# Attention work of two rounds in one group between runs of uncut projection tiles

## The chip, the cores and the metric

The kernel runs on one core of one Trainium2 chip. The metric is the device time of one execution in microseconds; less is better. Engines are named as in the profile: PE is TensorE's matmul side, DVE is VectorE, ACT is ScalarE, POOL is GpSimd, and SP is the queue that issues most transfers.

## The reference, cut to what matters

One decoder layer over 2048 tokens of width 1024, in float32. The changed part is the first sublayer:

```python
z = rms_norm(x, norm_g) @ w_in            # qa, ka, va, qr, kr, vr, gr, up
scores = einsum(qb, kk) * HEAD_DIM ** -0.5 + bias      # 128-token blocks: own and previous block
scores = where(valid, scores, NEG_INF)
m = maximum(scores.max(-1), sink)
p = exp(scores - m[..., None])
o = einsum(p, vv) / (p.sum(-1) + exp(sink - m))        # 6 query heads, 2 key/value heads
...
x = x + concat(o, retention(qr, kr, vr, gr), pool_mixer(up)) @ w_out
x = x + square(relu(rms_norm(x) @ w_up)) @ w_down
```

The retention part rotates `qr` and `kr` (rotary), and works on the same 128-token chunks.

## The kernel before

The mixer runs four passes (`q` = 0 to 3) over 512 tokens each, four blocks `b` of 128 tokens in a pass; the feed-forward part follows. Every product of the wide projections is done as three matmuls of split operands (`ring_hi`, `ring_lo`, `hT_hi`, `hT_lo`; L2174, L2175 and L2176), 128x512 each. In a pass PE first makes six tiles with `proj_T`, then twelve tiles G0 to G11 with `proj_G` (8 steps of three matmuls each, 96 steps in all), then one more `proj_T` tile (`T_UP1`), and then the sixteen `out_tile`s with the retention work between them. G tile t holds columns of group t // 4 (queries and keys of the retention, gate, values) for block t % 4.

The attention of a pass is eight rounds i: block b = i // 2, key/value head g = i % 2. Its steps are spread over the engines:

- PE: `att_scores(j)` (L2277) multiplies queries of block j // 2 with the previous (j even) or own (j odd) block's keys, into the two banks S0 and S1; `att_transposes(i)` (L2291) turns the weights of round i into T0 or T1; `att_out(b)` (L2305) multiplies the weights of a block with the values, into OB.
- DVE: scaling and bias (L1496), `row_stats(i)` (L1504 to L1511), `softmax(i)` (L1516 to L1522), `evac_pt(i)` (L1530), `yA_low(b)` (L1536).
- ACT: `exps(i)` (L1037, L1040), `yA_high(b)` (L1046).

Among these steps stand others. Weights come in units of 128x1024: SP loads a unit into one of three `stage` slots, ACT writes the high part (`split_hi`, L965), DVE the low part (`split_lo`, L1693); SP loads unit u only when `split_lo(u - 3)` is done, and `split_hi(u)` also waits until the last product with the unit that held its ring slot is done. ACT copies each G tile out of its bank (`evac_G`, L1029; there are three such banks) and makes tanh for the gate (`tanh_of`, L1068), DVE multiplies the gate (`gate_of`, L1574). The rotation of block b takes two POOL instructions (`rot_b`, L850) and two of DVE (`rot_a` L1544, `rot_add` L1549), and then POOL makes `kz_of(b)` (L857). `rot_b(b)` with b of 2 or 3 waits for `rot_add(b - 2)`. POOL's own order in a pass is rot_b(0), rot_b(1), rot_b(2), kz_of(0), kz_of(1), rot_b(3), windows(0) (two instructions, L892), kz_of(2), kz_of(3), windows(1).

Each engine runs its list in the order in which `mixer_pe`, `mixer_act`, `mixer_dve` and `mixer_pool` are written, and the engines meet only in semaphores. An instruction that waits holds up all that stand behind it on its engine. After the G tiles ACT has, in this order: `split_hi(22)`, `split_hi(23)`, `tanh_of(2)`, `tanh_of(3)`, `yA_high(3)`, `evac_qkT(0)` (L1059); PE has `proj_T(T_UP1)`, `att_out(3)`, `qk_transposes(0)` (L2320), `out_tile(0)`, and `ret_scores(0)` (L2334), which waits for `evac_qkT(0)`.

## Time and profile before

| | |
|---|---|
| device time, median of 3 runs | 2017.3 us (2016.82 to 2017.58) |
| the profiled execution: time / span | 2016.09 us / 2014.3 us |
| busy share of the span: PE, DVE, ACT, POOL | 99%, 70%, 44%, 9% |
| granted TensorE clock over the span | 0.999 |

Busy time of an engine is the union of its instructions' durations. A row of a timeline gives the start in microseconds from the start of the span, the duration from the first start to the last end of what is merged in it, and xN for N merged instructions; a matmul of 32-bit operands that isn't in the split form counts as two of PE's instructions for some shapes. Consecutive matmuls overlap in such rows, so PE is read from start to start. What stands in brackets is the engine's idle time before the row, and what ended it.

### The profile page before, as it was taken

Reading aid. Unit: us, or ns where it says so; the run is one execution under the profiler, and the core shown is the slowest. Engines: PE = TensorE matmul, PEld = TensorE weight load, DVE = VectorE, ACT = ScalarE, POOL = GpSimd, SP = SyncE. Lnnn points to the kernel's source line nnn. Section 1 sums busy time; section 2 is a strip of 40 time slices with the busy share of each in tenths; the row PEclk is TensorE's granted clock in tenths of the full one; section 3 lists DMA queues with packets and bytes.
Section 4 is the critical chain, followed back from the end, with each engine's and each line's share of the span. In section 5 each row is a group of like instructions: output and inputs, shape, how many; then the busy total and the mean of one; then the engine's idle time right before and its main releaser. Section 6 shows DMA issues by size and latency. Waiting matters only on the chain.

```text
span 2014.3 us, 26083 instructions
## 1 busy us (share of the span) xinstructions
PE 2002.5 (99%) x9580; PEld 1639.2 (81%) x9580; DVE 1405.4 (70%) x2043; ACT 886.5 (44%) x1484; POOL 181.8 (9%) x279
## 2 busy tenths in 40 slices
PE   9999999999999999999999999999999999999998
PEld 7778878877887788888888888888888888888886
DVE  5685577558746867777778767767666668667667
ACT  5343434444353436545446554445333334433333
POOL 2132122202320220000000000000000000000001
PEclk9999999999999999999999999999999999999999
DMA  8223422531352233576856557787947578756572
GB/s 281 64 95 136 142 64 75 193 105 63 97 191 84 94 115 101 147 190 161 179 148 142 147 146 180 178 195 196 403 188 282 196 292 331 285 198 265 197 290 84
DMA packets 101947, 348.60 MB, mean 173 GB/s; under 512 B 10267, under 2 KB 12220, under 8 KB 84412
## 3 DMA queue, kind: packets, MB, share of 16 engines
q1 hardware_dynamic: 99372, 338.27, 52.7%
q10 hardware_dynamic: 2448, 8.65, 1.2%
q8 instruction: 77, 1.26, 0.3%
q14 instruction: 50, 0.41, 0.1%
HBM read 270.21 MB, written 76.68 MB: 172 GB/s over the span
## 4 chain that ended last, share of the span: by engine, by line
PE 98%; DVE 1%; ACT 1%; issue 0%; POOL 0%; POOLq 0%; ACTq 0%
PE bank L2174 30%; PE bank L2176 30%; PE bank L2175 30%; PE bank L2277 1%; PE bank L2305 1%; PE bank L2353 1%; PE bank L2334 1%; PE bank L2356 1%; PE bank L2320 1%; PE bank L2396 1%; PE bank L2361 1%; PE bank L2291 1%; DVE hT_lo L1466 1%; PE bank L2381 0%; PE bank L2164 0%; PE bank L2371 0%
## 5 line engine op out<-in xcount | busy, mean ns | idle before, releaser
L2174 PE MATMUL bank<-h_hi,w_lo 128*128 128x512 f32 x912 | 355.7, 390 | 0.2 <-DVE h_lo L1677 0.2
L2176 PE MATMUL bank<-h_hi,w_hi 128*128 128x512 f32 x912 | 354.8, 389 | 0.0
L2175 PE MATMUL bank<-h_lo,w_hi 128*128 128x512 f32 x912 | 354.8, 389 | 0.0
L2174 PE MATMUL bank<-d_hi,u_lo 128*128 128x512 f32 x896 | 348.5, 389 | 0.0
L2175 PE MATMUL bank<-d_lo,u_hi 128*128 128x512 f32 x896 | 348.5, 389 | 0.0
L2176 PE MATMUL bank<-d_hi,u_hi 128*128 128x512 f32 x896 | 348.5, 389 | 0.0
L1309 ACT ACTIVATE u_hi<-u_raw 128x1024 fp32r<-128x1024 f32 x112 | 118.6, 1059 | 327.5 <-PE bank L2176 315.3
L1935 DVE TENSOR_TENSOR u_lo<-u_raw,u_hi 128x1024 fp32r<-128x1024 f32 x112 | 137.1, 1224 | 179.5 <-ACT u_hi L1309 179.5
L2174 PE MATMUL bank<-ring_hi,hT_lo 128*128 128x512 f32 x544 | 219.8, 404 | 0.0
L2176 PE MATMUL bank<-ring_hi,hT_hi 128*128 128x512 f32 x544 | 212.8, 391 | 0.0
L2175 PE MATMUL bank<-ring_lo,hT_hi 128*128 128x512 f32 x544 | 212.4, 390 | 0.0
L2176 PEld LDWEIGHTS bank<-h_hi,w_hi 128*128 128x128 f32 x912 | 171.2, 188 | 35.6
L2174 PEld LDWEIGHTS bank<-h_hi,w_lo 128*128 128x128 f32 x912 | 171.2, 188 | 35.4 <-issue 0.4
L2175 PEld LDWEIGHTS bank<-h_lo,w_hi 128*128 128x128 f32 x912 | 171.2, 188 | 35.3
L2176 PEld LDWEIGHTS bank<-d_hi,u_hi 128*128 128x128 f32 x896 | 168.2, 188 | 35.0
L2174 PEld LDWEIGHTS bank<-d_hi,u_lo 128*128 128x128 f32 x896 | 168.2, 188 | 34.9
L2175 PEld LDWEIGHTS bank<-d_lo,u_hi 128*128 128x128 f32 x896 | 168.2, 188 | 34.9
L1693 DVE TENSOR_TENSOR ring_lo<-stage,ring_hi 128x1024 fp32r<-128x1024 f32 x108 | 132.0, 1242 | 52.6 <-ACT ring_hi L965 52.0
L1686 DVE TENSOR_TENSOR w_lo<-wraw,w_hi 128x512 fp32r<-128x512 f32 x156 | 104.2, 687 | 76.0 <-ACT w_hi L1112 75.1
L965 ACT ACTIVATE ring_hi<-stage 128x1024 fp32r<-128x1024 f32 x108 | 110.7, 1053 | 72.6 <-DMA stage<-in_wmix 40.4
L1112 ACT ACTIVATE w_hi<-wraw 128x512 fp32r<-128x512 f32 x156 | 96.7, 626 | 91.8 <-PE bank L2176 86.9
L2174 PEld LDWEIGHTS bank<-ring_hi,hT_lo 128*128 128x128 f32 x544 | 102.2, 188 | 24.6 <-issue 2.4
(220 smaller groups left out, 3038.0 us busy)
## 6 DMA issues: line engine op xcount, KB each, us to landing
u_raw<-u_dram SPq DMA_DIRECT2D x56, 1024.0 KB, 4.8
d_raw<-in_wdn SPq DMA_DIRECT2D x56, 1024.0 KB, 6.9
stage<-in_wmix SPq DMA_DIRECT2D x108, 512.0 KB, 4.4
u_dram<-ur SPq DMA_DIRECT2D x32, 1280.0 KB, 9.6
wraw<-in_wup SPq DMA_DIRECT2D x128, 256.0 KB, 3.7
e_raw<-in_wdn SPq DMA_DIRECT2D x24, 1024.0 KB, 8.9
xq<-in_x SPq DMA_DIRECT2D x16, 512.0 KB, 3.6
x_dram<-xq ACTq DMA_DIRECT2D x16, 512.0 KB, 3.0
```

The source lines that it names most:

```text
L965: act.activation(ring_hi[:, SLOT[u % NU], :], stage[:, u % STAGE, :], ACT.Copy).then_inc(whi_done.sem, 1)
L1112: act.activation(w_hi[w_slot(n, k)][:, :, :].rearrange("p c n -> p (c n)"), w_source(n, k), ACT.Copy).then_inc(w_hi_done, 1)
L1309: act.activation(hi[:, cell, :], src[:, 2 * h:2 * h + 2, :], ACT.Copy).then_inc(m_hi_done, 1)
L1466: dve.scalar_tensor_tensor(out=hT_lo[:, c, :], in0=xT[:, c, :], scalar=gcol[:, c:c + 1], in1=hT_hi[:, c, :].bitcast(F32), op0=ALU.mult, op ...
L1686: dve.tensor_tensor(w_lo[s][:, :, :].rearrange("p c n -> p (c n)"), w_source(n, k), w_hi[s][:, :, :].rearrange("p c n -> p (c n)").bitcast ...
L1693: dve.tensor_tensor(ring_lo[:, s, :], stage[:, u % STAGE, :], ring_hi[:, s, :].bitcast(F32), ALU.subtract).then_inc(wlo_done.sem, 1)
L1935: dve.tensor_tensor(lo[:, cell, :], src[:, 2 * h:2 * h + 2, :], hi[:, cell, :].bitcast(F32), ALU.subtract).then_inc(m_lo_done, 1)
L2174: pe.matmul(dst, al, bh, start=(first and k == 0), stop=False, skip_group_check=chain)
L2175: pe.matmul(dst, ah, bl, start=False, stop=False, skip_group_check=chain)
L2176: last = pe.matmul(dst, ah, bh, start=False, stop=(final and k == n - 1), skip_group_check=chain)
L2277: last = pe.matmul((S0, S1)[g][:, P * h:P * h + P], qT[a:a + HEAD, h, b * P:(b + 1) * P], kT[a:a + HEAD, (b + e) * P:(b + e + 1) * P], sta ...
L2291: last = pe.transpose((T0, T1)[k][:, h * P:(h + 1) * P], score_buf(i // 2)[:, k, 256 * h:256 * h + P], ident[:, :])
```

## The change

The order of the G stage is written anew on PE, ACT and DVE. Before, PE cut the 96 steps of the G tiles into sixteen pieces of six; after the odd pieces stood `att_out` or `att_scores` or both, after the even ones the transposes of one round. Now 24 steps (three whole tiles) run in one piece, and behind each such piece stand all the attention steps of two rounds together: `att_scores(2b+2)`, the transposes of rounds 2b and 2b+1, `att_out(b-1)`, `att_scores(2b+3)`. Behind the last three tiles only the transposes of rounds 6 and 7 and `att_out(2)` are left. DVE and ACT handle the two rounds of a block one behind the other. On DVE the rotations of blocks 1, 2 and 3, which stood in rounds 5, 6 and 7, now all stand behind the softmax of round 7, with units 18 and 19 and the first gate among them, and ahead of `evac_pt(6)`. The instructions are the same ones, and as many. Two semaphores (`osb_done`, `sqr_done`) become one (`ret_read`) that counts both; `score_half` is renamed `score_part`.

The functions' diff, without the places where only the semaphore's name changes:

```diff
@@ -1070,12 +1069,12 @@
             def ret_out(q, b):
                 act.wait_ge(ro_done.sem, ro_done.now(q, b))
                 act.wait_ge(qktr_done.sem, qktr_done.now(q, 2 * b + 1))
-                act.activation(osb_view(b), OB[:, 0:384], ACT.Copy).then_inc(osb_done.sem, 1)
+                act.activation(osb_view(b), OB[:, 0:384], ACT.Copy).then_inc(ret_read.sem, 1)
                 if b:
                     act.wait_ge(ss6_done.sem, ss6_done.now(q, b - 1))
                 else:
                     act.wait_ge(o_done.sem, o_done.now(q, 3))
-                act.activation(sq, OB[:, 0:384], ACT.Square).then_inc(sqr_done.sem, 1)
+                act.activation(sq, OB[:, 0:384], ACT.Square).then_inc(ret_read.sem, 1)
 
             def yR_high(q, b):
                 act.wait_ge(ytr_done.sem, ytr_done.now(q, b))
...
@@ -1204,31 +1203,36 @@
                 split_hi(q, 11)
                 exps(q, 0)
                 evac_v(q)
-                for i in range(8):
-                    if i % 2:
-                        evac_G(q, 3 * (i // 2) + 1)
-                    if i == 2:
+                exps(q, 1)
+                for b in range(NB):
+                    if b == 1:
                         split_hi(q, 12)
                         split_hi(q, 13)
-                    if i in (2, 4, 6):
-                        yA_high(q, i // 2 - 1)
-                    if i == 3:
+                    if b >= 2:
+                        yA_high(q, b - 2)
+                    if b == 3:
+                        tanh_of(q, 0)
+                    if b:
+                        exps(q, 2 * b)
+                    evac_G(q, 3 * b)
+                    if b == 1:
                         split_hi(q, 14)
                         split_hi(q, 15)
-                    if i == 5:
+                    if b == 2:
                         split_hi(q, 16)
                         split_hi(q, 17)
-                    if i == 7:
+                    if b == 3:
+                        split_hi(q, 18)
+                        split_hi(q, 19)
                         tanh_of(q, 1)
+                    if b:
+                        exps(q, 2 * b + 1)
+                    evac_G(q, 3 * b + 1)
+                    if b == 3:
                         split_hi(q, 20)
                         split_hi(q, 21)
-                    if i < 7:
-                        exps(q, i + 1)
-                    evac_G(q, 3 * (i // 2) + 2 * (i % 2))
-                    if i == 6:
-                        split_hi(q, 18)
-                        split_hi(q, 19)
-                        tanh_of(q, 0)
+                    evac_G(q, 3 * b + 2)
+                yA_high(q, 2)
                 split_hi(q, 22)
                 split_hi(q, 23)
                 tanh_of(q, 2)
...
@@ -1716,53 +1720,58 @@
                 split_lo(q, 6)
                 split_lo(q, 7)
                 split_lo(q, 8)
-                score_half(q, 0)
+                score_part(q, 0)
                 split_lo(q, 9)
                 evac_scaled(q, 5)
                 split_lo(q, 10)
-                score_half(q, 1)
+                score_part(q, 1)
                 row_stats(q, 0)
+                row_stats(q, 1)
                 split_lo(q, 11)
-                for i in range(8):
-                    if i:
-                        evac_pt(q, i - 1)
-                    softmax(q, i)
-                    if i in (2, 5):
-                        split_lo(q, 12 if i == 2 else 16)
-                        split_lo(q, 13 if i == 2 else 17)
-                    if i in (2, 4, 6):
-                        yA_low(q, i // 2 - 1)
-                    if i < 6:
-                        score_half(q, i + 2)
-                    if i < 7:
-                        row_stats(q, i + 1)
-                    if i == 1:
-                        dve.wait_ge(sc_done.sem, sc_done.now(q, 3))
-                        dve.tensor_copy(bias0[:, :, 0:P], bias[:, :, 0:P]).then_inc(carried.sem, 1)
-                    if i == 3:
+                softmax(q, 0)
+                softmax(q, 1)
+                dve.wait_ge(sc_done.sem, sc_done.now(q, 3))
+                dve.tensor_copy(bias0[:, :, 0:P], bias[:, :, 0:P]).then_inc(carried.sem, 1)
+                for b in range(1, NB):
+                    score_part(q, 2 * b)
+                    evac_pt(q, 2 * b - 2)
+                    evac_pt(q, 2 * b - 1)
+                    score_part(q, 2 * b + 1)
+                    if b == 1:
+                        split_lo(q, 12)
+                        split_lo(q, 13)
+                    if b >= 2:
+                        yA_low(q, b - 2)
+                    row_stats(q, 2 * b)
+                    row_stats(q, 2 * b + 1)
+                    if b == 2:
                         split_lo(q, 14)
                         split_lo(q, 15)
-                    if i == 4:
+                        split_lo(q, 16)
+                        split_lo(q, 17)
+                    softmax(q, 2 * b)
+                    softmax(q, 2 * b + 1)
+                    if b == 2:
                         rot_a(q, 0)
                         rot_add(q, 0)
-                    if i == 5:
+                    if b == 3:
                         rot_a(q, 1)
                         rot_add(q, 1)
-                    if i == 6:
+                        split_lo(q, 18)
+                        split_lo(q, 19)
+                        gate_of(q, 0)
                         rot_a(q, 2)
                         rot_add(q, 2)
-                        split_lo(q, 18)
-                        split_lo(q, 19)
-                    if i == 7:
-                        gate_of(q, 0)
                         rot_a(q, 3)
                         rot_add(q, 3)
-                        evac_pt(q, 7)
-                        gate_of(q, 1)
-                        split_lo(q, 20)
-                        split_lo(q, 21)
-                        pool_first(q, 0)
-                        pool_rest(q, 0)
+                evac_pt(q, 6)
+                evac_pt(q, 7)
+                yA_low(q, 2)
+                split_lo(q, 20)
+                split_lo(q, 21)
+                gate_of(q, 1)
+                pool_first(q, 0)
+                pool_rest(q, 0)
                 split_lo(q, 22)
                 split_lo(q, 23)
                 gate_of(q, 2)
...
@@ -2412,14 +2421,16 @@
                 for b in range(NB):
                     last = pe.transpose(T0[:, b * P:(b + 1) * P], vT[:, b * P:(b + 1) * P], ident[:, :])
                 last.then_inc(vtr_done.sem, 1)
-                for i in range(8):
-                    proj_G(q, GSTEPS * i, GSTEPS * i + GSTEPS // 2)
-                    if i in (2, 4, 6):
-                        att_out(q, i // 2 - 1)
-                    if i < 6:
-                        att_scores(q, i + 2)
-                    proj_G(q, GSTEPS * i + GSTEPS // 2, GSTEPS * i + GSTEPS)
-                    att_transposes(q, i)
+                for b in range(NB):
+                    proj_G(q, 2 * GSTEPS * b, 2 * GSTEPS * b + 2 * GSTEPS)
+                    if b < NB - 1:
+                        att_scores(q, 2 * b + 2)
+                    att_transposes(q, 2 * b)
+                    att_transposes(q, 2 * b + 1)
+                    if b:
+                        att_out(q, b - 1)
+                    if b < NB - 1:
+                        att_scores(q, 2 * b + 3)
                 proj_T(q, T_UP1)
                 att_out(q, 3)
                 qk_transposes(q, 0)
```

PE's list at the group between G5 and G6. In the kernel after the change (`sc_odd` holds the weights of an odd block, `pt` the transposed ones):

```order
L2185 MATMUL bank<-ring_hi,hT_hi 128x512
L2286 MATMUL bank<-kT,qT 128x128 x6
L2300 MATMUL bank<-ident,sc_odd 128x128 x6
L2314 MATMUL bank<-pt,vtok 64x384 x4
L2286 MATMUL bank<-kT,qT 128x128 x6
L2183 MATMUL bank<-ring_hi,hT_lo 128x512
```

In the kernel before, the same work stands at two places of many, the end of `att_out(0)` with `att_scores(4)`, and one round's transposes:

```order
L2176 MATMUL bank<-ring_hi,hT_hi 128x512
L2305 MATMUL bank<-pt,vtok 64x384 x4
L2277 MATMUL bank<-kT,qT 128x128 x6
L2174 MATMUL bank<-ring_hi,hT_lo 128x512
```

```order
L2176 MATMUL bank<-ring_hi,hT_hi 128x512
L2291 MATMUL bank<-ident,sc 128x128 x3
L2174 MATMUL bank<-ring_hi,hT_lo 128x512
```

What was cut off by six steps of projection each time is now one piece, in which `att_scores` stands at both ends.

DVE's list behind the softmax of round 7, up to units 20 and 21. After the change (each pair of L1548 and L1553 is one rotation, L1697 is `split_lo`, L1578 the gate, L1534 `evac_pt`, L1540 `yA_low`):

```order
L1526 TENSOR_SCALAR sc_odd<-sc_odd,rinv 128x128 x3
L1548 TENSOR_TENSOR zt<-zt,tabs 128x768
L1553 TENSOR_TENSOR zt<-zt,rt 128x768
L1697 TENSOR_TENSOR ring_lo<-stage,ring_hi 128x1024 x2
L1578 SCALAR_TENSOR_TENSOR zt<-thb,zt 128x384
L1548 TENSOR_TENSOR zt<-zt,tabs 128x768
L1553 TENSOR_TENSOR zt<-zt,rt 128x768
L1548 TENSOR_TENSOR zt<-zt,tabs 128x768
L1553 TENSOR_TENSOR zt<-zt,rt 128x768
L1534 TENSOR_TENSOR pt<-bank,window 128x384 x4
L1540 TENSOR_TENSOR yA_lo<-bank,yA_hi 128x3x128
L1697 TENSOR_TENSOR ring_lo<-stage,ring_hi 128x1024 x2
```

Before (L1544 and L1549 the rotation, L1693 `split_lo`, L1574 the gate, L1530 `evac_pt`), from units 18 and 19 on:

```order
L1693 TENSOR_TENSOR ring_lo<-stage,ring_hi 128x1024 x2
L1530 TENSOR_TENSOR pt<-bank,window 128x384 x2
L1516 TENSOR_TENSOR rsum<-rsum,ses 128x3
L1518 RECIPROCAL rinv<-rsum 128x3
L1522 TENSOR_SCALAR sc_odd<-sc_odd,rinv 128x128 x3
L1574 SCALAR_TENSOR_TENSOR zt<-thb,zt 128x384
L1544 TENSOR_TENSOR zt<-zt,tabs 128x768
L1549 TENSOR_TENSOR zt<-zt,rt 128x768
L1530 TENSOR_TENSOR pt<-bank,window 128x384 x2
L1574 SCALAR_TENSOR_TENSOR zt<-thb,zt 128x384
L1693 TENSOR_TENSOR ring_lo<-stage,ring_hi 128x1024 x2
```

Three rotations now stand between the softmax of round 7 and `evac_pt(6)`, and `evac_pt(6)`, `evac_pt(7)` and `yA_low(2)` stand ahead of unit 20, where one rotation and `evac_pt(7)` stood.

ACT's list in the last block. After (L1028 is `evac_G`, L964 `split_hi`, L1067 tanh, L1036 and L1039 one round's exponentials, L1045 `yA_high`), from `evac_G(9)` to units 22 and 23:

```order
L1028 ACTIVATE zt<-bank,rstd 128x512
L964 ACTIVATE ring_hi<-stage 128x1024 x2
L1067 ACTIVATE thb<-zt 128x384
L1036 ACTIVATE sc_odd,rsum<-sc_odd,nmax 128x128 x3
L1039 ACTIVATE ses<-sde 128x3
L1028 ACTIVATE zt<-bank,rstd 128x512
L964 ACTIVATE ring_hi<-stage 128x1024 x2
L1028 ACTIVATE zt<-bank,rstd 128x512
L1045 ACTIVATE yA_hi<-bank 128x3x128
L964 ACTIVATE ring_hi<-stage 128x1024 x2
```

Before, from the exponentials of round 7 on:

```order
L1037 ACTIVATE sc_odd,rsum<-sc_odd,nmax 128x128 x3
L1040 ACTIVATE ses<-sde 128x3
L1029 ACTIVATE zt<-bank,rstd 128x512
L965 ACTIVATE ring_hi<-stage 128x1024 x2
L1068 ACTIVATE thb<-zt 128x384
L1029 ACTIVATE zt<-bank,rstd 128x512
L1068 ACTIVATE thb<-zt 128x384
L965 ACTIVATE ring_hi<-stage 128x1024 x2
L1029 ACTIVATE zt<-bank,rstd 128x512
L965 ACTIVATE ring_hi<-stage 128x1024 x2
```

The exponentials of round 7 moved behind `evac_G(9)`, units 18 and 19 and a tanh.

## Rows read from the trace of the kernel before

**Rows 1.** The page's chain of work that ended last, by engine.

```profile
PE 98%; DVE 1%; ACT 1%; issue 0%; POOL 0%; POOLq 0%; ACTq 0%
```

**Rows 2.** Spans and mean granted clock of the cores.

```profile
core 0: 2014.3 us, clock 0.999
```

**Rows 3.** Timeline of PE, pass 1: start, us, engine, line, operation [idle before].

```profile
198.49 0.39 PE L2174 MATMUL bank<-hT_hi,ring_lo 128*128 128x512 f32 x1
...
203.70 0.39 PE L2176 MATMUL bank<-hT_hi,ring_hi 128*128 128x512 f32 x1
...
234.91 0.48 PE L2174 MATMUL bank<-ring_hi,hT_lo 128*128 128x512 f32 x1
...
290.20 0.94 PE L2277 MATMUL bank<-kT,qT 64*128 64x128 f32 x12
...
314.30 0.48 PE L2174 MATMUL bank<-hT_hi,ring_lo 128*128 128x512 f32 x1
...
319.94 1.51 PE L2305 MATMUL bank<-pt,vtok 128*64 128x384 f32 x8
321.39 0.88 PE L2320 MATMUL bank<-ident,zt 128*128 128x128 f32 x6
322.02 0.48 PE L2174 MATMUL bank<-ring_hi,yA_lo 128*128 128x512 f32 x1
...
324.26 0.60 PE L2334 MATMUL bank<-sc 64*128 64x128 f32 x6
```

**Rows 4.** Timeline of DVE, pass 1, the steps of the group.

```profile
249.82 1.14 DVE L1496 SCALAR_TENSOR_TENSOR sc_odd<-bank,rstd,bias 128x384 f32<-128x384 f32 x2 [2.98 <-PE bank L2277]
...
284.19 0.95 DVE L1544 TENSOR_TENSOR zt<-zt,tabs 128x768 f32<-128x768 f32 x1
...
286.20 1.02 DVE L1530 TENSOR_TENSOR pt<-bank,window 128x384 f32<-128x384 f32 x2
...
315.51 0.55 DVE L1574 SCALAR_TENSOR_TENSOR zt<-thb,zt 128x384 f32<-128x384 f32 x1
315.98 2.35 DVE L1693 TENSOR_TENSOR ring_lo<-stage,ring_hi 128x1024 fp32r<-128x1024 f32 x2
...
324.48 0.55 DVE L1536 TENSOR_TENSOR yA_lo<-bank,yA_hi 128x384 fp32r<-128x384 f32 x1
```

**Rows 5.** Timeline of ACT, pass 1.

```profile
304.06 0.40 ACT L1037 ACTIVATE sc_odd<-sc_odd,nmax 128x128 f32<-128x128 f32 x1 [2.18 <-DVE nmax L1508]
...
305.33 0.67 ACT L1029 ACTIVATE zt<-bank,rstd 128x512 f32<-128x512 f32 x1
305.90 2.00 ACT L965 ACTIVATE ring_hi<-stage 128x1024 fp32r<-128x1024 f32 x2
307.79 0.51 ACT L1068 ACTIVATE thb<-zt 128x384 f32<-128x384 f32 x1
...
320.70 1.06 ACT L965 ACTIVATE ring_hi<-stage 128x1024 fp32r<-128x1024 f32 x1 [4.81 <-DMA stage<-in_wmix]
...
322.87 0.86 ACT L1059 ACTIVATE sc<-bank 128x384 f32<-128x384 f32 x2
```

**Rows 6.** Timeline of POOL, pass 1.

```profile
297.55 0.83 POOL L857 TENSOR_TENSOR kz<-zt,small 128x384 f32<-128x384 f32 x1 [8.15 <-DVE zt L1549]
298.34 2.32 POOL L850 TENSOR_TENSOR rt<-zt,tabs 128x384 f32<-128x384 f32 x2
300.61 1.06 POOL L892 TENSOR_TENSOR qT<-up 128x527 f32<-128x527 f32 x1
...
326.93 1.92 POOL L892 TENSOR_TENSOR qT<-qT 128x521 f32<-128x521 f32 x1
```

**Rows 7.** Timeline of DVE at the same moments, and one L1522 apart from them.

```profile
298.72 3.04 DVE L1522 TENSOR_SCALAR sc_odd<-sc_odd,rinv 128x128 f32<-128x128 f32 x3
...
310.59 0.68 DVE L1522 TENSOR_SCALAR sc_odd<-sc_odd,rinv 128x128 f32<-128x128 f32 x3
...
326.46 1.47 DVE L1693 TENSOR_TENSOR ring_lo<-stage,ring_hi 128x1024 fp32r<-128x1024 f32 x1
```

More of the change, by code:

```diff
@@ L1480, in evac_scaled, with score_part @@
                                          op0=ALU.mult, op1=ALU.mult).then_inc(s_evac.sem, 1)
-            def score_half(q, j):
+            def score_part(q, j):
                 b, e = j // 2, j % 2
@@ L1577, in ret_ya @@
             def ret_ya(q, b):
-                dve.wait_ge(osb_done.sem, osb_done.now(q, b))
+                dve.wait_ge(ret_read.sem, ret_read.now(q, 2 * b))
                 dve.wait_ge(gate_done.sem, gate_done.now(q, b))
@@ L2298, in att_out @@
                 else:
[L2299 to L2300 removed]
+                    pe.wait_ge(ret_read.sem, ret_read.before(q, 7))
+                    pe.wait_ge(ret_read.sem, ret_read.before(q, 6))
                     pe.wait_ge(v_evac.sem, v_evac.now(q, 3))
@@ L2344, in ret_outs @@
                     pe.wait_ge(R_done.sem, R_done.now(q, 2 * b - 1))
-                    pe.wait_ge(sqr_done.sem, sqr_done.now(q, b - 1))
+                    pe.wait_ge(ret_read.sem, ret_read.now(q, 2 * b - 1))
                 else:
```

13 lines of the change are left out of this document (5 added, 8 removed).

## The prediction

> **What bounds the kernel now.** I read the chain of work that ended last first: PE is 98% of it [rows 1], at a granted clock of 0.999 [rows 2]. So the time is PE's own list plus its waits, and DVE, ACT, POOL and the transfers count only where PE comes to wait for them. Then I read PE's timeline in pass 1 [rows 3]. A projection tile without interruption has 23 starts from 198.49 to 203.70, that is 0.2265 us for each 128x512 matmul, and 5.44 us for a tile of 24. The stage that the change rewrites, from the first G matmul at 234.91 to the first of T_UP1 at 314.30, lasts 79.4 us. Its 288 projection matmuls need 65.2. PE's idle time is nowhere visible in it, and the other three passes repeat it; the remaining 14.2 us are attention work and what each change between the two kinds of work costs.
>
> **The gain: fewer interruptions.** A score set (six matmuls, 12 records) is 0.94 long, about 0.88 from start to start; an output set is 1.45 (319.94 to 321.39), and six transposes 0.63 (321.39 to 322.02), so three are 0.32 [rows 3]. The stage holds 6 score sets, 3 output sets and 8 sets of three transposes: 5.3 + 4.35 + 2.55 = 12.2 us. So 14.2 - 12.2 = 2.0 us go to 15 interruptions. The change leaves 4. If all cost alike (0.13 each), 11 fewer save 1.5 us. If those with transposes alone cost nothing, the 2.0 fall on the seven others (0.28 each), of which four remain, and the saving is 0.85. I take 1.1 us per pass, near the middle, 4.4 in all. The attention work stays. The joined semaphore costs nothing: ACT issues both of its increments in the old order, and nobody waits for a later one than before.
>
> **The first new wait: the second score set.** In the group behind G2, `att_scores(3)` writes the banks that `score_part(2)` must have read. That takes DVE 1.14 us for its two halves, begun as soon as the scores are there [rows 4] (its first row: DVE had been idle for 2.98 us until the scores ended). DVE is free then. With about 0.1 for each hand-over this is 1.3 us, and between the two score sets PE has only six transposes, 0.63. Wait: 0.7 us. In the groups behind G5 and G8 `att_out` adds 1.45 to the cover, so 2.1 against 1.3, and there is none. Behind the waiting PE stand the next 72 projection matmuls.
>
> **The second new wait: DVE's tail of the last block.** Let t = 0 be the start of G9. The tile ends at 5.6 (5.44 and about 0.1 for the change-over). ACT's list has `evac_G(9)`, units 18 and 19, a tanh and only then the exponentials of round 7. From [rows 5]: 0.2 until the copy starts, 0.57 (305.33 to 305.90), 1.89 (to 307.79), 0.5, and 1.27 (304.06 to 305.33) give t = 10.0. DVE's other work for round 7 is done before that: evac_pt(4) and (5), a score part, yA_low and two row statistics are under 7 us from t = -0.8. The softmax needs 1.1 (its three scalings are 0.68 [rows 7]) and ends at 11.1 to 11.2. One rotation is 2.0 us (284.19 to 286.20), so that of block 1 ends at 13.2.
>
> Behind it DVE has, until unit 20 is done: units 18 and 19 (2.35), a gate (0.47, 315.51 to 315.98), two rotations (4.0), evac_pt(6) and (7) (1.02 each with 0.08 overlap, 1.9), yA_low(2) (0.5), unit 20 (1.2) [rows 4]: 10.4 us. So unit 20 is done at t = 23.6 if nothing disturbs DVE.
>
> But the rotation of block 1 also releases POOL: kz_of(1) 0.83, rot_b(3) 2.32, windows(0) 2 x 1.06, and kz_of(2) 0.83 behind the next rotation [rows 6], 6.1 us, all of it now beside DVE instructions that read two SBUF operands. The trace shows what that costs. Three scalings took 3.04 us instead of 0.68 while POOL ran its two rot_b instructions and a window (298.34 to 301.7) [rows 6, 7]: each waited for one POOL instruction. In the other direction the POOL window of 326.93 took 1.92 instead of 1.06, while DVE split a unit from 326.46 on, and that split took 1.47 instead of 1.2. So the two take turns, and the one that waits waits nearly to the other's end. Seven such DVE instructions stand behind unit 18's start; with six POOL instructions between them, each 0.15 less than its length (the split's small delay), 5.2 us are added and unit 20 is done at 28.8. If DVE keeps its turn as long as it has work, it comes to `rot_a(3)` at 17.9, which waits for kz_of(1) and rot_b(3), 3.2 us, and then alternates with the windows: 27.8. I take 28.3. Nothing at all would be 23.6.
>
> The Trainium skill speaks against this change here: SBUF — State Buffer, section Who interferes with whom, says that a Vector instruction with two SBUF inputs and a GpSimd instruction that reads SBUF exclude each other for their whole length. By that rule the tail is the serial sum, close to 28.8; by the durations alone it is 23.6. The trace agrees with the rule but for about 0.15 us of overlap.
>
> What that does to PE: SP may load unit 23 only when unit 20 is done. Before, unit 20 was done at about 317.15 (315.98 and half of 2.35), ACT began unit 23 at 320.70 with a transfer as what it had waited for, and ended evac_qkT(0) at 323.73 (322.87 and 0.86) [rows 4, 5]. So `ret_scores(0)` can start 6.6 us after unit 20. PE wants it at 324.26, which is 9.96 behind the start of T_UP1 [rows 3]. In the new order T_UP1 starts at 16.4 (three tiles and a change-over) + 0.63 + 1.45 + 0.1 = 18.6, so PE wants the scores at 28.6. They can start at 28.3 + 6.6 = 34.9: wait 6.3 us (6.8 and 5.8 for the two orders of turns, 1.6 without turns). About half of it shows earlier, as a wait of `att_out(3)` for evac_pt(7) and yA_low(2), which end near 27.1 where PE wants them at 24.2; the sum is the same. Afterwards DVE reaches the decay products of chunk 0 about 9.8 us behind unit 20, and PE wants them 10.3 behind it, so no third wait follows. Behind the waiting `ret_scores(0)` stand all of the output tiles; nothing in them could take the lost time back, since PE has no idle time there to give.
>
> **The other moves.** In block 1 and 2 the same ACT order delays the odd round's exponentials, but PE wants the weights only at 17.7: block 1 ends its softmax near 14.2, or 16.2 if its scalings wait for rot_b(0). In block 2 unit 17 is late (it is loaded behind unit 14, which now stands behind the row statistics): the softmax ends at about 14.6, the rotation at 16.6, and score_part(6) can start at 17.5. Both are covered, by 0.9 us or more. Cover gone, each costs its lateness and no more. Transfers keep their number and order on SP.
>
> **The sum.** Per pass: -1.1 + 0.7 + 6.3 = +5.9 us; four passes: +23.6. The profiled execution has 2016.09, so 2039.7 for such a one. The median of the runs shown is 1.2 higher, hence 2040.9, say 2041.
>
> **The rivals.** *DVE and POOL run side by side* (or POOL's instructions find gaps): -1.1 + 0.7 + 1.6 per pass, +4.8, 2022. For it: DVE's split lost only 0.27 to POOL; against it: the 3.04 and the 1.92. Chance 0.17. *The tail is covered* (the end wait doesn't come, since the list is faster than I add up by 2 us or more; it needs unit 20 done by t = 22.0): -0.4 per pass, 2015.7, no change. Against it: the 10.4 us are durations in rows, and the start at 13.2 hangs on a whole G tile. Chance 0.06. *The change does what it says and is faster*: the place is the change-over at each of the 11 removed interruptions, the price up to 2.0 us per pass for all 15; with unit 20 by 22.0 and no wait at the second scores it gives 4 x -1.1, 2012.9, and decides only when both waits together stay under 0.1 us per pass. Chance 0.03. *Worse than forecast*: the pauses of 3 us in PE could bring the granted clock down, from 0.999 now [rows 2]; the work between the two pauses, 4.3 us (319.94 to 324.26), would then take twice as long at 1.2 GHz, +17, 2058; or the tail delays a further step by a microsecond or two. The trace has no such pause to judge by. Chance 0.12. My forecast, with 5.8 to 6.8 us and an own range of 2036 to 2045, has 0.62.
>
> **How the numbers follow.** Faster or slower by 0.2% (4 us) is about what a measurement of this kernel can tell. Faster: 0.03. Same: the covered tail and the low part of the first rival, 0.10. Slower: the rest, 0.87. The range reaches from 2021 (the first rival) to 2048; outside are the covered tail, the faster case and the clock.
>
> **What would show each step.** In the changed kernel's profile the chain should hold some 25 us of DVE, ACT, POOL and a transfer. Each pass should have a pause of 0.7 us between the scores of round 2 and 3, a G stage about 0.4 us shorter, up to T_UP1, and pauses that end in att_out(3) and in the first retention scores, 6.3 together. DVE's rotations of blocks 2 and 3 should be stretched to 1.5 us and more an instruction, or POOL's windows. If they are as short as now and the end pause is under 2 us, the turns were the failed step. If PE waits in the groups behind G5 or G8, I have missed a dependency, and if the clock reads under 0.99, the pauses cost more than themselves.

## The result, and the profile after

The changed kernel takes 2042.9 us (median of 4 runs, 2040.9 to 2045.7) against 2017.4 (2016.8 to 2017.7): ratio 1.0129, 95% interval 1.0117 to 1.0142. It is slower by 1.3%, 25.5 us; 2041 was forecast. The profiled execution took 2040.93 with a span of 2039.1, against 2016.09 and 2014.3. In its profile line 1540 stands for 1536, 1697 for 1693, 2286 for 2277 and so on: DVE's lines moved by 4, PE's by 9, ACT's and POOL's by -1.

The page's chain of work that ended last, by engine (before in [rows 1]):

```profile
PE 90%; DVE 5%; DMA 2%; ACT 2%; issue 1%; POOL 0%; ACTq 0%; POOLq 0%; SPq 0%; DVEq 0%
```

The waits of PE over the whole span: line that waited, engine and line it waited for, us in total, times, longest.

```profile
PE bank L2314 <- DVE yA_lo L1540: 9.0, 4, 2.3
PE bank L2343 <- ACT sc L1058: 7.9, 4, 2.9
PE bank L2173 <- POOL ones L800: 2.8, 1, 2.8
PE bank L2286 <- DVE sc_odd L1500: 1.8, 4, 0.4
```

The chain holds far more outside PE than the 25 us that the prediction named as a sign (2% of the span before, 10% now, some 160 us more): it doesn't follow the delay alone. In pass 1 it leaves PE at the end of G9 and comes back only at `ret_scores(0)`.

Of the four waits three are new, four times each, once a pass: `att_out(3)`, `ret_scores(0)` and the second score set. The third line (2.8 us, once) stands before too. PE's timeline in pass 1 shows where they are (compare [rows 3]):

```profile
257.33 0.94 PE L2286 MATMUL bank<-kT,qT 64*128 64x128 f32 x12
258.20 0.88 PE L2300 MATMUL bank<-ident,sc 128*128 128x128 f32 x6
259.52 0.94 PE L2286 MATMUL bank<-kT,qT 64*128 64x128 f32 x12 [0.44 <-DVE sc_odd L1500]
...
328.15 1.75 PE L2314 MATMUL bank<-pt,vtok 128*64 128x384 f32 x8 [2.25 <-DVE yA_lo L1540]
329.83 1.54 PE L2329 MATMUL bank<-ident,zt 128*128 128x128 f32 x6
...
335.93 1.51 PE L2343 MATMUL bank<-sc 64*128 64x128 f32 x12 [1.81 <-ACT sc L1058]
```

DVE's timeline in the same pass, from the last softmax to unit 20 (compare [rows 4]):

```profile
311.94 0.68 DVE L1526 TENSOR_SCALAR sc_odd<-sc_odd,rinv 128x128 f32<-128x128 f32 x3
312.53 0.95 DVE L1548 TENSOR_TENSOR zt<-zt,tabs 128x768 f32<-128x768 f32 x1
313.52 0.96 DVE L1553 TENSOR_TENSOR zt<-zt,rt 128x768 f32<-128x768 f32 x1
314.40 2.99 DVE L1697 TENSOR_TENSOR ring_lo<-stage,ring_hi 128x1024 fp32r<-128x1024 f32 x2
317.31 1.54 DVE L1578 SCALAR_TENSOR_TENSOR zt<-thb,zt 128x384 f32<-128x384 f32 x1
318.77 1.93 DVE L1548 TENSOR_TENSOR zt<-zt,tabs 128x768 f32<-128x768 f32 x1
320.73 1.70 DVE L1553 TENSOR_TENSOR zt<-zt,rt 128x768 f32<-128x768 f32 x1
322.36 1.81 DVE L1548 TENSOR_TENSOR zt<-zt,tabs 128x768 f32<-128x768 f32 x1
324.21 1.47 DVE L1553 TENSOR_TENSOR zt<-zt,rt 128x768 f32<-128x768 f32 x1
325.60 1.94 DVE L1534 TENSOR_TENSOR pt<-bank,window 128x384 f32<-128x384 f32 x4
327.46 0.54 DVE L1540 TENSOR_TENSOR yA_lo<-bank,yA_hi 128x384 fp32r<-128x384 f32 x1
327.93 2.34 DVE L1697 TENSOR_TENSOR ring_lo<-stage,ring_hi 128x1024 fp32r<-128x1024 f32 x2
```

The first rotation, with POOL idle, takes 0.95 and 0.96; the next two, beside POOL, 1.93, 1.70, 1.81 and 1.47. POOL's timeline at the same time (compare [rows 6]):

```profile
314.56 1.75 POOL L856 TENSOR_TENSOR kz<-zt,small 128x384 f32<-128x384 f32 x1 [13.88 <-DVE zt L1553]
316.26 3.62 POOL L849 TENSOR_TENSOR rt<-zt,tabs 128x384 f32<-128x384 f32 x2
319.85 1.77 POOL L891 TENSOR_TENSOR qT<-up 128x527 f32<-128x527 f32 x1
321.70 1.66 POOL L891 TENSOR_TENSOR qT<-qT 128x525 f32<-128x525 f32 x1
323.32 1.54 POOL L856 TENSOR_TENSOR kz<-zt,small 128x384 f32<-128x384 f32 x1
325.76 0.83 POOL L856 TENSOR_TENSOR kz<-zt,small 128x384 f32<-128x384 f32 x1 [0.90 <-DVE zt L1553]
```

Each is stretched to its own length plus a good part of one DVE instruction (kz 1.75 and 1.54 for 0.83), except the last, which falls beside mask copies that read PSUM (0.83). Behind unit 20 (done at 329.13) stands, in the chain of waits of this stretch (start, us, what), the transfer of unit 23, and behind that ACT, pass 1:

```profile
328.00 1.14 DVE ring_lo L1697
...
329.16 3.67 DMA stage<-in_wmix
```

```profile
332.86 1.06 ACT L964 ACTIVATE ring_hi<-stage 128x1024 fp32r<-128x1024 f32 x1 [10.31 <-DMA stage<-in_wmix]
...
335.02 0.86 ACT L1058 ACTIVATE sc<-bank 128x384 f32<-128x384 f32 x2
```

**A balance for each pass.** From PE's rows I read two lengths: G, from the first G matmul to the first of T_UP1, and the end, from there to `ret_scores(0)`. Before they are 79.39 and 9.96 in every pass (within 0.01), 89.35 together. After they are 79.33 and, over the four passes, 15.65, 15.81, 15.46 and 15.55: sums 94.97, 95.14, 94.79 and 94.87. That is 22.4 us more in four passes, of the 24.8 by which the span grew. PE's waits are not all of it: those of `att_out(3)` and `ret_scores(0)` are 16.9 us. In passes 0 to 2 the work between the two pauses, 4.3 us long before, ran in part at half the clock (last section), and PE would have waited for ACT in that time anyway. All experiments below are read with this balance; the runs' medians are set beside it.

### The profile page after: what moved, and what is told of

The parts are those of the page before. It is cut to its first block, busy times and chain, and to the rows that moved or that the text cites. A ratio compares the mean times of both kernels' runs of the same rounds, so it can differ in the third digit from the quotient of the medians.

```text
span 2039.1 us, 26082 instructions
## 1 busy us (share of the span) xinstructions
PE 2008.6 (99%) x9580; PEld 1646.4 (81%) x9580; DVE 1405.2 (69%) x2043; ACT 886.2 (43%) x1484; POOL 197.5 (10%) x279
## 4 chain that ended last, share of the span: by engine, by line
PE 90%; DVE 5%; DMA 2%; ACT 2%; issue 1%; POOL 0%; ACTq 0%; POOLq 0%; SPq 0%; DVEq 0%
PE bank L2183 28%; PE bank L2185 28%; PE bank L2184 28%; PE bank L2286 1%; DVE ring_lo L1697 1%; PE bank L2362 1%; DVE zt L1548 1%; DMA d_raw<-in_wdn 1%; PE bank L2343 1%; DMA stage<-in_wmix 1%; PE bank L2365 1%; PE bank L2314 1%; PE bank L2405 1%; DVE zt L1553 1%; PE bank L2370 1%
## 5 line engine op out<-in xcount | busy, mean ns | idle before, releaser
L2183 PE MATMUL bank<-ring_hi,hT_lo 128*128 128x512 f32 x544 | 215.4, 396 | 0.0
L2185 PEld LDWEIGHTS bank<-d_hi,u_hi 128*128 128x128 f32 x896 | 168.2, 188 | 34.9
L1697 DVE TENSOR_TENSOR ring_lo<-stage,ring_hi 128x1024 fp32r<-128x1024 f32 x108 | 134.7, 1267 | 57.4 <-ACT ring_hi L964 56.9
L964 ACT ACTIVATE ring_hi<-stage 128x1024 fp32r<-128x1024 f32 x108 | 111.6, 1055 | 130.6 <-DMA stage<-in_wmix 75.8
```

The costliest lines, as they stand in the source:

```text
L964: act.activation(ring_hi[:, SLOT[u % NU], :], stage[:, u % STAGE, :], ACT.Copy).then_inc(whi_done.sem, 1)
L1697: dve.tensor_tensor(ring_lo[:, s, :], stage[:, u % STAGE, :], ring_hi[:, s, :].bitcast(F32), ALU.subtract).then_inc(wlo_done.sem, 1)
L2183: pe.matmul(dst, al, bh, start=(first and k == 0), stop=False, skip_group_check=chain)
L2185: last = pe.matmul(dst, ah, bh, start=False, stop=(final and k == n - 1), skip_group_check=chain)
```

## The experiments

The kernel before ran beside each: 2016.75 us with the first four runs, 2016.64 with e5 to e8, 2016.92 with e9 and e10, 2016.82 with e11. The diffs are cut: of a step that moved they show where it went, and mostly not the line that it left.

**e1: POOL's instructions made short.** In passes 1 to 3 `kz_of(1)`, `kz_of(2)`, `rot_b(3)` and `windows(0)` work on a small part of their data (128x64, 128x32); the rest of it isn't computed, so the time alone is read.

```diff
-                src = zt[:, b, 0:768].rearrange("p (h i two) -> p h i two", h=12, two=2)
+                nh = 1 if q and b == 3 else 12
+                src = zt[:, b, 0:64 * nh].rearrange("p (h i two) -> p h i two", h=nh, two=2)
...
+                nh = 1 if q and b in (1, 2) else 6
...
+                    hi = lo + 32 if q and cc == 0 else PADW + QT
```

> The changed kernel, but in passes 1 to 3 the five POOL instructions that fall beside the last block's tail on DVE work on a small part of their data: both of rot_b(3) and kz_of(1) and kz_of(2) on one head, windows(0) on 32 columns (their results are incomplete; pass 0 is as it was). Turns between DVE and POOL (my theory): DVE's way from the end of the rotation of block 1 to unit 20 was 14.6 us in the changed kernel against 10.4 by its durations; it should fall to 10.7 to 11.2 in passes 1 to 3, and 3 x 3.7 = 11 us go: 2032 us. DVE and POOL side by side (rival): that way is long for another reason, nothing changes: 2043. In both cases pass 0 keeps its pauses.

2027.1 us, ratio 1.0051 (1.0036 to 1.0066), 5 us below the forecast of 2032. DVE's timeline, pass 1:

```profile
314.79 2.45 DVE L1700 TENSOR_TENSOR ring_lo<-stage,ring_hi 128x1024 fp32r<-128x1024 f32 x2
317.16 0.62 DVE L1581 SCALAR_TENSOR_TENSOR zt<-thb,zt 128x384 f32<-128x384 f32 x1
317.70 1.02 DVE L1551 TENSOR_TENSOR zt<-zt,tabs 128x768 f32<-128x768 f32 x1
318.76 0.96 DVE L1556 TENSOR_TENSOR zt<-zt,rt 128x768 f32<-128x768 f32 x1
...
323.86 2.35 DVE L1700 TENSOR_TENSOR ring_lo<-stage,ring_hi 128x1024 fp32r<-128x1024 f32 x2
```

Same DVE list, same place, and every instruction has nearly its bare length again. From the end of rotation 1 to the end of unit 20 pass 10.2 us where the changed kernel took 14.65: the turns cost 4.4. The end is 11.22, 11.08 and 11.02 in the three edited passes, and 15.62 in pass 0, which kept POOL's work, in the same execution. The three differences are 13.5 of the 15.8 us gained against the changed kernel; that the 1.6 us of low clock in its pass 1 (last section) are absent here fits the rest.

**e2: two rotations earlier.** Rotations 1 and 2 stand between the softmaxes of rounds 6 and 7, where DVE waits for ACT.

```diff
                     softmax(q, 2 * b)
+                    if b == 3:
+                        rot_a(q, 1)
+                        rot_add(q, 1)
+                        rot_a(q, 2)
+                        rot_add(q, 2)
                     softmax(q, 2 * b + 1)
```

> The changed kernel, with the rotations of blocks 1 and 2 on DVE moved ahead of the softmax of round 7, where DVE had waited 3.4 us for the exponentials. My theory with turns: kz_of(1), rot_b(3) and windows(0) come beside the softmax (its three scalings take about 3 us then, as in the kernel before) and the units 18 and 19; unit 20 is done 2.6 us earlier in each pass, 2032 us. Without turns the tail would be 7 us shorter, the pauses at the end would vanish: 2019.

2025.6 us, ratio 1.0046 (1.0031 to 1.0061). Unit 20 starts at 320.35, 4.1 behind T_UP1 where it was 7.8, and the end is 11.85, 1.9 more than before:

```profile
328.09 0.94 PE L2344 MATMUL bank<-sc 64*128 64x128 f32 x12 [1.75 <-ACT sc L1058]
```

The turns are still there (units 18 and 19 took 3.85 at 311.93), but in part in time that DVE had stood idle. Of the two cases expected, the truth is in the middle: unit 20 came 3.7 us earlier, not 2.6.

**e3: unit 20 alone earlier**, behind the first gate and ahead of rotation 2:

```diff
                         gate_of(q, 0)
+                        split_lo(q, 20)
                         rot_a(q, 2)
```

> The changed kernel, with unit 20's low part on DVE moved from behind yA_low(2) to ahead of the rotation of block 2. Unit 23 is then loaded long before it is wanted. If the late load alone made the pause (rival), all of the end wait goes: -5.8 us per pass, 2020. If the tail has two exits, as I hold, evac_pt(7) and yA_low(2) only end about 1.1 us later, att_out(3) waits that much longer, and the retention scores come 0.7 us earlier: 2040.

2040.2 us, ratio 1.0118 (1.0103 to 1.0133). Unit 20 is done 8 us sooner, and the tail's length now shows in full at the next user of DVE:

```profile
329.19 1.90 PE L2314 MATMUL bank<-pt,vtok 128*64 128x384 f32 x8 [3.39 <-DVE yA_lo L1540]
...
335.11 0.94 PE L2343 MATMUL bank<-sc 64*128 64x128 f32 x12
```

So the transfer of unit 23 isn't the bottleneck by itself; DVE's list is. But the time came out as forecast partly by luck. `ret_scores(0)` no longer waits for anything (ACT's copy for it ends at 333.09), so the end should be the late `att_out(3)` plus the 4.3 us of PE's own work between the two, 13.5 (an estimate from 329.19, the start of T_UP1 at 320.02 and 4.32 before), 2.1 less than the changed kernel's mean. It is 14.93, 15.09, 16.24 and 15.02, because that work took 5.8 to 7.1 us: behind the pause of 3.39 the granted clock fell in all four passes. In pass 1:

```profile
330.00:332.00 2.00, 2.00 (x11) 1.01 (x7) 1.87 (x7) 0.94 (x3) 0.00 (x0) 0.54 0.32 57
332.00:334.00 2.00, 2.00 (x8) 1.69 (x7) 1.94 (x3) 1.22 (x3) 0.00 (x0) 0.61 0.51 205
```

(The columns are explained in the last section; the clock is the third number from the end.) The earlier unit is worth about 2 us a pass, and the low clock took most of that back.

**e4: the exponentials of round 7 earlier**, right behind those of round 6 on ACT:

```diff
                     if b:
                         exps(q, 2 * b)
+                    if b == 3:
+                        exps(q, 7)
                     evac_G(q, 3 * b)
```

> The changed kernel, with the exponentials of round 7 on ACT moved to stand right behind those of round 6, ahead of the copy of G9, units 18 and 19 and a tanh. My theory: the whole tail on DVE starts 3.2 us earlier and the end wait is 3.2 us shorter in each pass: -12.9, 2030. If the pause came from a transfer or from PE itself, ACT's order would not matter: 2043.

2029.9 us, ratio 1.0067 (1.005 to 1.0084), as forecast. The softmax of round 7 ends 8.0 behind the start of G9 and not 11.1, and the end is 12.46, 3.35 less than in the changed kernel, and 2.5 more than before.

**e5: all rotations out of the tail**, 0 at the end of block 1, 1 between units 15 and 16, 2 behind the softmax of round 5, 3 between the softmaxes of block 3:

```diff
                         split_lo(q, 15)
+                        rot_a(q, 1)
+                        rot_add(q, 1)
...
                     softmax(q, 2 * b)
+                    if b == 3:
+                        rot_a(q, 3)
+                        rot_add(q, 3)
                     softmax(q, 2 * b + 1)
+                    if b < 3:
+                        rot_a(q, 2 if b == 2 else 0)
+                        rot_add(q, 2 if b == 2 else 0)
```

> One edit: the four rotations leave the tail of the last block and go where VectorE stands idle in the trace of the changed kernel: rotation 0 to the end of block 1 (idle 271.9 to 274.8), rotation 1 between the lower halves of units 15 and 16 in block 2 (idle 1.7), rotation 2 behind the softmax of round 5, rotation 3 between the two softmaxes of block 3. The exponentials of round 7 stay late (10.0 us behind the start of the last group). My theory (the block of rotations with its turns against GpSimd makes unit 20 late): the softmax of round 7 ends 11.2 behind the group's start as now, units 18 and 19, gate 0, the mask copies (from 17.0, when the attention outputs are ready) and unit 20 follow, done near 20.8 to 21.5, against 27.6 now and 10.4 wanted at least; the start of T_UP1 is at 18.6, so unit 20 is done 2.5 us behind it and the first retention scores can start 9.1 to 9.5 behind it, against 9.96 of the kernel before: no wait is left, and the time is before minus 0.75 a pass, near 2014.5 us. Rival (the late exponentials are the cause and the rotations only ride behind them): a wait of 2 to 4 us a pass stays, 2023 to 2030 us. Rival (GpSimd's work only moves and stretches the softmaxes of block 2): att_scores of block 3 come late, above 2025 us.

2027.0 us, ratio 1.0052 (1.0039 to 1.0064): 12 us above my forecast. The end is right (10.39), but G is 81.47 for 79.33. The third case of the expectation came, in which GpSimd's work only moves; e6 shows where.

**e6: the same, with exponentials 7 early (as e4) and units 20 and 21 ahead of the mask copies.**

> The rotations spread as in the run beside it, the exponentials of round 7 right behind those of round 6 on ScalarE, and the lower halves of units 20 and 21 ahead of the four mask copies. Unit 20 is then done near 16 us behind the start of the last group, more than 2 us ahead of T_UP1. If the rotations alone had set the end wait this changes nothing against the run beside it: 2014.5 us, within 1 us. If the late exponentials or the mask copies kept a part of the wait, it is faster than the run beside it by that part, up to 8 us.

2025.4 us, ratio 1.0044 (1.0031 to 1.0056), 11 us above the forecast. The end is 10.02, without a wait, and G is 81.54: the 9 us are all in block 2. PE's timeline, pass 1, the group behind G8:

```profile
296.53 0.55 PE L2301 MATMUL bank<-ident,sc 128*128 128x128 f32 x3 [0.45 <-DVE sc L1528]
...
299.44 0.94 PE L2287 MATMUL bank<-kT,qT 64*128 64x128 f32 x12 [0.93 <-DVE sc_odd L1502]
```

DVE ahead of it:

```profile
283.20 3.34 DVE L1699 TENSOR_TENSOR ring_lo<-stage,ring_hi 128x1024 fp32r<-128x1024 f32 x2
286.47 1.94 DVE L1550 TENSOR_TENSOR zt<-zt,tabs 128x768 f32<-128x768 f32 x1
288.44 1.47 DVE L1555 TENSOR_TENSOR zt<-zt,rt 128x768 f32<-128x768 f32 x1
289.84 2.98 DVE L1699 TENSOR_TENSOR ring_lo<-stage,ring_hi 128x1024 fp32r<-128x1024 f32 x2
292.75 1.13 DVE L1522 TENSOR_TENSOR rsum<-rsum,ses 128x3 f32<-128x3 f32 x1
```

The turns moved with the work. Rotation 0 at the end of block 1 had let POOL run `rot_b(2)` beside units 14 and 15 (3.34 for 2.35), rotation 1 let it run `kz_of(1)` and `rot_b(3)` beside units 16 and 17 and the softmax: even a sum of 128x3 took 1.13 for 0.16.

**e7: the same, and the scores of round 3 behind two projection steps of the next group.**

```diff
+                    if b == 1:
+                        proj_G(q, g, g + 2)
+                        att_scores(q, 3)
+                        proj_G(q, g + 2, g + 2 * GSTEPS)
```

> As the run beside it with everything early, and the scores of round 3 are issued behind the first two projection steps (six matmuls) of the next group, not right behind the transposes of rounds 0 and 1. Theory: TensorE no longer waits for the score part of round 2 (0.44 us of wait and its restart, 0.69 in all a pass), but the group is interrupted once more (0.07 to 0.14): 0.5 us a pass less than the run beside it, 2 us in all, near 2012.5 us, read from the length of the twelve G tiles (79.3 now, 78.8 then). Rival (the wait was hidden in the drain of the transposes): the same length as the run beside it or 0.1 more.

2023.2 us, ratio 1.0034 (1.0021 to 1.0046): G 81.00, 0.54 less than e6, the wait of 0.44 gone. The 0.5 a pass came as expected, on top of block 2's loss, which e7 shares with e6; so the total is 11 us above its forecast.

**e8: the same as e6, and `att_out(0)`, (1), (2) in the middle of their groups.**

```diff
+                        proj_G(q, g, g + GSTEPS)
+                        att_out(q, b - 1)
+                        proj_G(q, g + GSTEPS, g + 2 * GSTEPS)
```

> As the run with everything early, and the attention outputs of blocks 0, 1 and 2 are issued in the middle of a group of 24 steps and not between two groups: three interruptions of the projection more a pass, twelve in all, nothing less. It prices one interruption by itself. If the saving of the change came from 11 interruptions less a pass (0.75 + 0.69 of wait = 1.44 a pass, 0.13 each), this costs 0.4 us a pass, 1.6 us in all, near 2016 us, and the G tiles of a pass take 0.4 us longer. Rival (an interruption costs nothing and the saving came from the transposes being six in a row): no longer than the run beside it.

2027.8 us, ratio 1.0057 (1.0041 to 1.0072), G 82.00. Its forecast of 2016 was 12 us too low, for the reason that e6 shows, and the 0.46 more in G doesn't price an interruption: with the outputs gone from between the two score sets, the scores of round 5 now wait 0.44 as those of round 3 do, and those of round 7 wait 1.48 for 0.93 in e6. It shows instead that `att_out` was the cover there, as the prediction had it.

**e9: fitted.** As e7, with rotation 0 between units 15 and 16, 1 behind the softmax of round 5, 2 between those of block 3, 3 behind gate 0.

```diff
                         split_lo(q, 15)
+                        rot_a(q, 0)
+                        rot_add(q, 0)
...
                     softmax(q, 2 * b)
+                    if b == 3:
+                        rot_a(q, 2)
+                        rot_add(q, 2)
                     softmax(q, 2 * b + 1)
+                    if b == 2:
+                        rot_a(q, 1)
+                        rot_add(q, 1)
```

> As the run that spreads the rotations, with early exponentials of round 7, unit 20 first and the scores of round 3 behind two projection steps, but block 2 carries two rotations in place of three: rotation 0 between units 15 and 16 (not at the end of block 1), rotation 1 behind the softmax of round 5, rotation 2 between the softmaxes of block 3, rotation 3 behind gate 0 where VectorE stood idle for 2.8 us. My theory (the 9 us that were left came from block 2, where VectorE's rotation and lower halves took turns with GpSimd's sines: 3.34 for 2.35, 1.94 and 1.47 for 0.95 and 0.96, 2.98 for 2.35, the first sum of the softmax 1.13 for 0.16, so that the transposes of round 5 waited 0.45 and the scores of round 7 0.93): the softmax of round 5 ends near 293 behind a start of T_UP1 at 317, both waits of TensorE are gone, the end stays without one, and the kernel takes 2016.7 - 4 x 0.75 - 4 x 0.5 = 2011.7 us. Rival (GpSimd's sines of block 2 collide with the lower halves of units 16 and 17 all the same): a wait of 0.5 to 1.5 a pass stays at the transposes of round 5 or the scores of round 7, 2014 to 2018 us.

2014.7 us, ratio 0.9989 (0.998 to 0.9998). G is 78.84 and the end 10.02 in all four passes, 0.49 less than before in each, 2.0 in all; the medians are 2.2 apart. PE's waits are those that stood there before (the longest here, the others 0.2 each):

```profile
PE bank L2176 <- POOL ones L800: 2.8, 1, 2.8
```

The forecast of 2011.7 was 3 us too low. It counted 0.5 for the wait on top of a saving of 0.75 a pass; the trace gives 0.49 for both together.

**e10: the same, with the scores of rounds 2, 4 and 6 in the middle of their groups** (round 3 back behind the transposes), so 7 interruptions of the stage for 5.

```diff
+                    proj_G(q, g, g + GSTEPS)
+                    if b < NB - 1:
+                        att_scores(q, 2 * b + 2)
+                    proj_G(q, g + GSTEPS, g + 2 * GSTEPS)
```

> As the run beside it, but the scores of rounds 2, 4 and 6 are issued in the middle of their groups of 24 steps, and those of round 3 right behind the transposes again. It prices an interruption without a wait hanging on it: two more a pass than the run beside it. By the 0.26 us that the attention outputs cost in the middle of a group (19.13 for 17.43, of which 1.44 is their own work) the twelve G tiles are 0.5 longer, less what the scores no longer wait: near 2013.5 us. Rival (0.13 an interruption, as 1.44 a pass by 11): 0.26 longer, near 2012.7 us. If VectorE's later score parts make a new wait, above 2015 us.

2015.7 us, ratio 0.9994 (0.9985 to 1.0004), G 79.07, no wait in it: 0.23 for two interruptions, 0.115 each. That is the expectation's second case (0.26), not the 0.5 of the first.

**e11: the changed kernel with its rotations placed as in e9, and nothing else.**

> The changed kernel with one edit: its rotations stand as in the fitted run (0 between units 15 and 16, 1 behind the softmax of round 5, 2 between the softmaxes of block 3, and 3, which the tail keeps, behind gate 0). The exponentials of round 7 stay late, unit 20 behind the mask copies, the scores of round 3 right behind the transposes. By the sums over a pass that have matched the times so far (G tiles plus the stretch from T_UP1 to the first retention scores, against 89.35 us of the kernel before): the G tiles take 79.33 as in the changed kernel, the end 10.0 to 10.8, since the tail holds 2 us of one rotation and unit 20 comes 3 to 4 us behind the start of T_UP1; 89.3 to 90.1 a pass, 2016.9 - 0 to + 3, taken 2018 us. Rival (the late exponentials of round 7 alone are worth a wait of 2 us or more a pass): above 2025 us.

2018.2 us, ratio 1.0007 (0.9998 to 1.0016), against 2018 expected. G is 79.32 and the end 10.30 to 10.44. Round 7's exponentials are as late as in the changed kernel and cost nothing more. This one edit on DVE gives back 24 of the 25.5 us.

Balance and times side by side, pass 1 (us; e1's pass 0 kept its long end):

| kernel | G | end | (G + end - 89.35) x 4 | median less before |
|---|---|---|---|---|
| changed | 79.33 | 15.81 | 23.2 | 25.5 |
| e2 | 79.32 | 11.85 | 7.3 | 8.9 |
| e3 | 79.32 | 15.09 | 20.2 | 23.5 |
| e4 | 79.32 | 12.46 | 9.7 | 13.1 |
| e5 | 81.47 | 10.39 | 10.0 | 10.3 |
| e6 | 81.54 | 10.02 | 8.8 | 8.7 |
| e7 | 81.00 | 10.02 | 6.7 | 6.6 |
| e8 | 82.00 | 9.99 | 10.6 | 11.1 |
| e9 | 78.84 | 10.02 | -2.0 | -2.2 |
| e10 | 79.07 | 10.02 | -1.0 | -1.2 |
| e11 | 79.32 | 10.30 | 1.1 | 1.4 |

The balance leaves at most 0.5 us open from e5 on, 1.6 in e2, and 2.3 to 3.4 in the changed kernel, e3 and e4, where PE's pauses are longest. Part of that rest is the clock: behind `ret_scores(0)`, so outside both lengths, it cost 1.6 us in the changed kernel, 0.8 in e3 and 3.0 in e4 (below).

## Why the prediction was right, step by step

*The gain.* Forecast 1.1 a pass, mis-sized: e9's G (78.84, no wait in it) less one interruption of 0.115 gives 78.72 for the changed kernel without a wait, so 11 interruptions less were worth 0.67. The step that failed is "the attention work stays", with 0.32 for three transposes. The starts in the rows show it. Before, three transposes among projection matmuls take 0.24, and the matmul behind them comes 0.1 late:

```profile
244.30 0.49 PE L2291 MATMUL bank<-ident,sc 128*128 128x128 f32 x3
244.54 0.48 PE L2174 MATMUL bank<-ring_hi,hT_lo 128*128 128x512 f32 x1
244.86 0.39 PE L2175 MATMUL bank<-ring_lo,hT_hi 128*128 128x512 f32 x1
```

In the changed kernel six transposes ahead of the outputs take 0.81 and not twice 0.24:

```profile
277.82 0.88 PE L2300 MATMUL bank<-ident,sc_odd 128*128 128x128 f32 x6
278.63 1.51 PE L2314 MATMUL bank<-pt,vtok 128*64 128x384 f32 x8
```

Added up over G in pass 1, the delays of the projection matmuls themselves (0.14 at a set of transposes, 0.21 at scores or outputs) fell from 2.6 to 0.8 us, 1.8 less and more than I had reckoned. But the 24 transposes took 3.7 us where they had taken 1.9: 0.56 of that is the wait at the second scores (1.31 for 0.75), and 1.2 is the price of their new neighbours, which I had put at nothing. 1.8 less 1.2 is the 0.6 to 0.7 gained. Why a transpose holds up scores or outputs longer than it holds up a projection matmul is not shown.

*The wait at the second scores.* Forecast 0.7: 79.33 - 78.72 = 0.6, of which the trace shows 0.44 as idle. e7 took it away and got 0.54 with an interruption more. The groups behind G5 and G8 had no wait, as forecast, and e8 showed for the one behind G5 that `att_out` is why.

*The tail.* Its start (the softmax of round 7 at t = 10.0 to 11.1 behind the start of G9, 301.47) came as forecast. Unit 20 was done at t = 27.7 where 28.3 was forecast; the turns cost 4.4 (e1 against the changed kernel), within the 4.2 to 5.2 (27.8 and 28.8, less 23.6). From unit 20 to the retention scores it took 6.8 for 6.6, so these started at 34.5 for 34.9: the end grew by 5.85 in pass 1 and 5.65 in the mean, for 6.3. The part at `att_out(3)` was 2.25, for 2.9. This mechanism is shown, not only argued: e1 takes the turns away and leaves DVE's list as it is, e2 and e11 take rotations from behind the softmax. Of its three parts no single one is the cause: without the late exponentials (e4) 2.5 of 5.85 stay, without the turns (e1) 1.1 to 1.3, and with unit 20 first (e3) 3.5 would stay at full clock. They are one serial DVE list, whose start, length and place of use add up. e11 shows that the list's length is what the change itself brought: with rotations elsewhere the late exponentials have slack.

*The sum.* Forecast -1.1 + 0.7 + 6.3 = 5.9 a pass; measured -0.67 + 0.6 + 5.65 = 5.6. Four times 5.6 is 22.4, plus 1.6 us of low clock in pass 1; 0.8 of the 24.8 in the span is unassigned. That 2041 came within 2 us of 2042.9 is partly luck: the gain was put 0.4 a pass too high and the tail 0.65 too long, which nearly cancel, and the low clock behind `ret_scores(0)` was not in the sum. The sign "a G stage about 0.4 us shorter" came as 0.06. The rival "side by side" fell with the stretched rows and with e1. The rival of the clock was right in kind and too large in size: the work between the two pauses did run slowly in three passes, but PE had to wait for ACT there anyway, so it cost nothing in the changed kernel. Where that wait is gone, in e3, the same work at low clock cost 1.4 to 2.8 us a pass.

The Trainium skill, SBUF — State Buffer, section Who interferes with whom, has the two kinds of instruction exclude each other for their whole length. The trace agrees in kind: 6.1 us of POOL's work [rows 6] added 4.4 to DVE's list, so near three quarters of it and not all. In the prediction's terms each POOL instruction cost 0.3 less than its length, not 0.15. The strict serial sum is 29.7 (23.6 and 6.1), not the 28.8 that the prediction gave for that rule, and 27.7 was measured.

## What to carry to other kernels

Work that is moved behind one long wait becomes a serial list, and its end is what matters: before gathering, add up the list from the moment at which its first input comes, with every release of another engine that it makes. A rotation that frees GpSimd to read SBUF cost, in these traces, its own time and much of GpSimd's as well, so move such steps to where neither engine's later work hangs on them (e5 looked at VectorE's idle time alone and lost 9 us in another block; e9 left GpSimd one stretched pair there, 4.17 us for 2.32, and PE waited for nothing). A switch of TensorE between kinds of work delays the projection by 0.14 to 0.21 us here, but what the small matmuls cost depends on what they stand next to: of 1.8 us a pass, 1.2 went back to the transposes and 0.6 to one new wait.

## What the hardware showed beyond that

**The clock after a pause.** Windows of the changed kernel, pass 1: PE busy and its count, weight loads, DVE, ACT, POOL, granted clock, DMA share, GB/s.

```profile
326.00:328.00 2.00, 0.00 (x0) 0.00 (x0) 2.00 (x6) 0.00 (x0) 0.59 (x1) 1.00 0.00 0
328.00:330.00 2.00, 1.85 (x9) 0.75 (x10) 2.00 (x3) 0.00 (x0) 0.00 (x0) 0.82 0.00 0
330.00:332.00 2.00, 2.00 (x8) 1.83 (x9) 1.87 (x7) 0.00 (x0) 0.00 (x0) 0.50 0.74 254
...
336.00:338.00 2.00, 2.00 (x15) 1.78 (x16) 2.00 (x5) 0.82 (x1) 1.03 (x1) 0.53 1.00 322
```

After PE had stood still for 2.25 us the clock fell to 0.50, that is 1.2 of 2.4 GHz; six transposes took 1.54 us for 0.87. After the pause of 1.75 in e2 they took 0.87. The same pause doesn't always do it: `att_out(3)` waited 2.25 us in all four passes and the clock fell in passes 0, 1 and 2, while in pass 3 it read 1.00 throughout, as it did in pass 0 of e1 (2.26). It fell in none of the four passes of e2 (pauses of 1.71 to 1.85), in two of four of e4 (2.33 to 2.47) and in all four of e3 (3.39). The second fall, behind `ret_scores(0)`, is what costs in the changed kernel: the way from there to `pool_mix(0)` is 6.33 us in passes 0, 2 and 3 and 7.92 in pass 1, and 7.79 and 7.92 in two passes of e4; in three passes of e3 it is 6.51 to 6.67. Why it comes in some passes only stays open, and so whether the wider spread of the changed kernel's runs (2040.9 to 2045.7) is due to it.

**Turns don't need size.** In e1 POOL's instructions on 128x32 and 128x64 elements still spanned 0.9 to 1.2 us, about the length of the DVE instruction that they stood beside, while DVE lost almost nothing to them. And in e2 and e6 DVE instructions of 0.16 us spanned 1.13 to 1.15 beside `rot_b`. In these rows what is short waits for what is long.
